# Splits of a norm, or of the mixer's output, woven into the first slabs of the product that reads them

## What is computed

```
for l in range(2):
    last = l == 1
    # context rows: all of it in layer 0, only the keys and values in layer 1
    hc = modulate(rms_norm_2(x_ctx, norm1_g[l]), cmod[0], cmod[1])
    hl = modulate(rms_norm_2(x_lat, norm1_g[l]), sh1, sc1)       # x * (1 + scale) + shift
    pa, q, k, v, pc = project(hl, P, rope)                       # hl @ w_in, 1024 x 2560
    o = diff_attn(q, k_all, v_all, lam)                          # 4 heads, two softmaxes each
    ya = chunk_gmlp(pa); yb = rms_norm_2(o, subln_g) * c; yc = conformer_conv(pc)
    x_lat = x_lat + g1 * (concat([ya, yb, yc]) @ w_out)          # 1024 x 1024
    h2 = modulate(rms_norm_2(x_lat, norm2_g[l]), sh2, sc2)
    x_lat = x_lat + g2 * ((silu(dwconv(h2 @ w_gate)) * (h2 @ w_val)) @ w_down)   # 2816 wide
```

## Time and profile before

| what | value |
|---|---|
| median of 3 runs | 2446.95 us |
| lowest and highest run | 2436.7 and 2447.53 us |
| profiled execution | 2444.05 us, of it the span 2442.4 us |
| TensorE matmul busy | 2222.0 us, 91% of the span |
| VectorE, ScalarE, GpSimd busy | 58%, 44%, 12% |
| mean granted TensorE clock | 0.948 of full speed |
| second block | from about 1348 us to the end |

### The profile page before, as it was taken

One profiled execution on the slowest core, in us unless ns is written; L12 is line 12 of the kernel. 1 busy time (PEld: TensorE's weight loads), 2 busy tenths in 40 slices (PEclk: granted clock), 3 DMA queues, 4 the chain that ended last, 5 costly groups with the idle time before them and its releaser, 6 DMA issues. The chain is left out here.

```text
span 2442.4 us, 31205 instructions
## 1 busy us (share of the span) xinstructions
PE 2222.0 (91%) x11948; PEld 1803.7 (74%) x11948; DVE 1421.3 (58%) x2234; ACT 1063.3 (44%) x1753; POOL 304.7 (12%) x310
## 2 busy tenths in 40 slices
PE   8998999899999989899999797789999998778999
PEld 6776677778777766777787675567888886658987
DVE  4655485554456555755454598755555337866664
ACT  4444555444344434554444454523232225454342
POOL 0007121100000062221000073100000001500000
PEclk9998999999999989999999898789999999889999
DMA  7553334466556534345656321222333334234654
GB/s 234 185 179 133 117 129 142 157 214 203 199 188 210 167 118 142 97 144 175 236 170 192 130 69 52 70 69 70 104 129 97 124 99 147 69 105 131 202 174 149
DMA packets 171842, 349.28 MB, mean 143 GB/s; under 512 B 11824, under 2 KB 23216, under 8 KB 171696
## 3 DMA queue, kind: packets, MB, share of 16 engines
q1 hardware_dynamic: 171696, 347.29, 43.7%
HBM read 346.19 MB, written 1.05 MB: 142 GB/s over the span
## 5 line engine op out<-in xcount | busy, mean ns | idle before, releaser
L820 DVE TENSOR_TENSOR wlo<-wraw,whi 128x1024 fp32r<-128x1024 f32 (+1 forms) x538 | 646.0, 1214 | 712.9 <-ACT whi L1017 710.9
L1017 ACT ACTIVATE whi<-wraw 128x1024 fp32r<-128x1024 f32 (+1 forms) x552 | 557.7, 1026 | 603.7 <-PE psum L1773 280.0
L1773 PE MATMUL psum<-whi,act_h 128*128 128x512 f32 (+2 forms) x1424 | 578.7, 406 | 30.4 <-DVE wlo L820 21.8
L1773 PE MATMUL psum<-wlo,act_h 128*128 128x512 f32 (+2 forms) x1424 | 557.4, 391 | 0.0
L1773 PE MATMUL psum<-whi,act_l 128*128 128x512 f32 (+2 forms) x1424 | 557.1, 391 | 0.0
L1773 PEld LDWEIGHTS psum<-whi,act_h 128*128 128x128 f32 x1424 | 275.6, 194 | 100.2 <-DVE wlo L820 25.6
L1773 PEld LDWEIGHTS psum<-whi,act_l 128*128 128x128 f32 x1424 | 274.4, 193 | 57.7
L1773 PEld LDWEIGHTS psum<-wlo,act_h 128*128 128x128 f32 x1424 | 275.4, 193 | 48.7
L1773 PE MATMUL psum<-act_h,whi 128*128 128x512 f32 (+1 forms) x704 | 243.8, 346 | 14.8 <-DVE cacc L1395 6.3
L1773 PE MATMUL psum<-act_l,whi 128*128 128x512 f32 (+1 forms) x704 | 239.6, 340 | 0.0
L1773 PE MATMUL psum<-act_h,wlo 128*128 128x512 f32 (+1 forms) x704 | 239.1, 340 | 0.0
(11 more groups left out here) (268 smaller groups left out, 2772.8 us busy)
## 6 DMA issues: line engine op xcount, KB each, us to landing
wraw<-in_w_in SPq DMA_DIRECT2D x136, 512.0 KB, 4.4
wraw<-in_w_gate SPq DMA_DIRECT2D x104, 512.0 KB, 4.2
wraw<-in_w_mod_pieces SPq DMA_DIRECT2D x96, 512.0 KB, 4.7
wraw<-in_w_ffn_in SPq DMA_DIRECT2D x80, 512.0 KB, 4.4
wraw<-in_w_ffn_out SPq DMA_DIRECT2D x44, 512.0 KB, 4.1
wraw<-in_w_down SPq DMA_DIRECT2D x44, 512.0 KB, 4.3
wraw<-in_w_val SPq DMA_DIRECT2D x40, 512.0 KB, 4.2
wraw<-in_w_branch SPq DMA_DIRECT2D x32, 512.0 KB, 4.8
```

The source lines that it names most:

```text
L820: eng.tensor_tensor(wlo[:, i, 0:st.n, 0:st.w], wraw[:, st.s % RING_W, 0:st.n, 0:st.w], whi[:, i, 0:st.n, 0:st.w].bitcast(F32), ALU.subtrac ...
L1017: nc.scalar.activation(whi[:, d % RING_S, 0:st.n, 0:st.w], wraw[:, s % RING_W, 0:st.n, 0:st.w], ACT.Copy).then_inc(sem("slab_rounded"), 1)
L1773: return nc.tensor.matmul(out, lhsT, rhs, start=start, stop=stop)
```

## The change

The splits are no longer all ahead of the product: four stand before its first slab, two before the second, two before the third (`between`), at all six places. `w_out_2` takes its slabs in the order in which its splits are made, k = 0, 6, 2, 4 (`order`), in both column groups. The count of product banks is set to 0 ahead of the feed-forward part, so that the first group of `w_gate_2` has banks 0 to 3, which no split uses; all later groups rotate from there. By the same count `w_down_2` then begins with banks 0 and 1, the banks of the last group of `w_val_2`, in both layers. In the attention, `subln`, `subln_root` and `subln_scale` move from right behind `att2_v` to the end of the round, behind `att2_t`, `att2_e` and `att2_m`. The number and shape of the instructions and loads are the same.

```diff
-def gemm(pl, weight, layer, act, tiles, nk, col0, width, evac, row0=0, kt0=0, ready=(), turned=False, **more):
+def gemm(pl, weight, layer, act, tiles, nk, col0, width, evac, row0=0, kt0=0, ready=(), turned=False, order=None, **more):
 
     steps = []
+    order = order or range(0, nk, SLAB_K)
...
-        for k in range(0, nk, SLAB_K):
+        for at, k in enumerate(order):
             n = min(SLAB_K, nk - k)
-            last = k + n == nk
+            last = at == len(order) - 1
...
-            pl.steps += ss
-            return {st.k: [("mod_lo", st.lo)] for st in ss}
-
-        ready = norm(0, 4, l > 0)
+            return {st.k: [("mod_lo", st.lo)] for st in ss}, between(ss)
+
+        def between(ss):
+
+            return [(0, st) for st in ss[:4]] + [(1, st) for st in ss[4:6]] + [(2, st) for st in ss[6:]]
+
+        ready, ss = norm(0, 4, l > 0)
...
-        others = [(5, cglu), (6, ct)] + [(at, st) for at, st in zip((7, 7, 11, 12, 12, 17, 17, 18), parts)]
+        others = ss + [(5, cglu), (6, ct)] + [(at, st) for at, st in zip((7, 7, 11, 12, 12, 17, 17, 18), parts)]
...
         for i in range(len(units) + 3):
+            behind = []
...
                 if kind == "att2_v":
-                    att += pending[:1]
+                    behind += pending[:1]
                     del pending[:1]
                     if h == B_HEADS - 1:
                         subs.append(Step(kind="subln", l=l, t=t, n=pl.tick("subs"), waits=drained(st.banks[0])))
-                        att.append(subs[-1])
+                        behind.append(subs[-1])
                         for part in ("subln_root", "subln_scale"):
                             pending.append(Step(kind=part, l=l, t=t, n=subs[-1].n))
+            att += behind
         att += pending
...
-            pl.steps += out
-
-        residual("w_out_2", "act2", KD, 0, {st.k: drained(st.bank) for st in ss}, True)
-
-
-        ready = norm(1, T, True)
+            pl.steps += weave(out, others)
+
+        residual("w_out_2", "act2", KD, 0, {st.k: drained(st.bank) for st in ss}, True, between(ss), order[::SLAB_K])
+
+
+        ready, ss = norm(1, T, True)
         pl.mod_queue, pl.mod_every, pl.mod_since = [(l, c) for c in MOD_GATES[1]], 5, 0
         base = pl.now("hid_lo")
-        pl.turns = tuple(range(7))
+        pl.turns, pl.gemm_banks = tuple(range(7)), 0
         for c, (a, w) in enumerate(widths(FFN)):
             n0 = pl.now("hid_lo")
             for weight, evac in (("w_gate_2", "ffg"), ("w_val_2", "ffv")):
-                pl.steps += gemm(pl, weight, l, "act2", T, KD, a, w, evac, ready=ready, turned=True, n0=n0)
-                ready = ()
+                pl.steps += weave(gemm(pl, weight, l, "act2", T, KD, a, w, evac, ready=ready, turned=True, n0=n0), ss)
+                ready = ss = ()
```

More of the change, by code:

```diff
@@ L171, in gemm @@
             banks.append(pl.gemm_bank())
-        for k in range(0, nk, SLAB_K):
+        for at, k in enumerate(order):
             n = min(SLAB_K, nk - k)
-            last = k + n == nk
+            last = at == len(order) - 1
             st = Step(kind="slab", s=len(pl.slabs), weight=weight, layer=layer, row=row0 + k, n=n, col=col0 + a, w=w,
-                      act=act, kt=kt0 + k, tiles=tiles, banks=banks, first=k == 0, last=last, c=c, a=a, evac=evac,
+                      act=act, kt=kt0 + k, tiles=tiles, banks=banks, first=at == 0, last=last, c=c, a=a, evac=evac,
                       turned=turned, **more)
@@ L181, in gemm @@
                 st.ready = [w for i in range(n) for w in ready.get(k + i, [])]
-            elif c == 0 and k == 0:
+            elif c == 0 and at == 0:
                 st.ready = list(ready)
@@ L197, in gemm @@
             elif (pl.mod_queue or pl.mod_last) and tiles == 2 and st.s >= 3 * RING_W:
-                at, slabs_in = k // SLAB_K, -(-nk // SLAB_K)
-                if pl.mod_queue and at % 4 == 0 and at + 3 < slabs_in:
+                if pl.mod_queue and at % 4 == 0 and at + 3 < len(order):
                     st.after = mod_ride(pl, pl.next_bank())
@@ L540, in plan_second, with residual @@
                    hi=pl.tick("split2_hi")) for k in order]
-        pl.steps += ss
-        def residual(weight, act, nk, g, ready, summed):
-            out = gemm(pl, weight, l, act, T, nk, 0, D, "res", ready=ready, g=g)
+        def residual(weight, act, nk, g, ready, summed, others=(), order=None):
+            out = gemm(pl, weight, l, act, T, nk, 0, D, "res", ready=ready, g=g, order=order)
             for st in out:
```

## The result

| | before | after |
|---|---|---|
| median of 20 runs | 2438.82 us | 2448.66 us |
| lowest and highest | 2429.39 and 2447.53 | 2443.7 and 2460.91 |
| span of the profiled execution | 2442.4 | 2447.8 |
| mean granted TensorE clock | 0.948 | 0.951 |

The changed kernel takes 1.0038 of the time of the one before, 95% interval 1.0027 to 1.0049: 9.3 us more (6.6 to 12.0). So the change is real, and smaller than the half per cent (12.2 us) that the prediction took as the least that tells from no change.

A forecast was written before the change was run, and what follows sets the result against it. TensorE, busy for 91% of the span, was taken as the bound, with VectorE the slower engine in the splits. The terms +4.5 - 4.5 + 3.0 + 1.8 + 0.35 + 1.9 - 4.0 made +3.0 us on 2446.95: 2450 us, range 2438 to 2460.

The forecast's parts named there:

- the band to which I gave 0.5: Whole kernel: 2445 to 2453 us, with no two terms at their far ends; chance 0.5.
- the clock rival: Woven products: broken starts keep TensorE at 1.2 GHz a whole slab longer than taken; +12.4, 2459 us; chance 0.1.
- first `w_in_2`: Layer 0: start 1.6 us earlier, two chains 4.8 later, clock 1.25 slower; sum 4.5 us slower.
- first `w_gate_2` and `w_down_2`: Layer 0: `w_gate_2` net 4.5 us faster, its slab 0 starting 8.1 earlier; `w_down_2` 0.5 later for a bank's drain.
- second `w_in_2`: Start 1.6 us earlier, slab 3's 1.2 delay gone, chains of 3.05 and 2.85, nothing for the clock; net 3.0 slower.
- second `w_gate_2` and `w_down_2`: Layer 1: `w_gate_2` 1.8 us slower from two chains of 1.45; `w_down_2` 1.4 later, waiting for a bank's drain.
- attention and `w_out_2`, twice: Attention 4 us faster from its new order; `w_out_2` 0.25 slower at the first place, 0.1 at the second.
- The chains: Slabs 1 and 2 wait for transposes, scaling and low part of a split; 2.4 us each at four tiles.
- The start of slab 0: Behind norms: 1.6 us earlier at each `w_in_2`, 8.1 at the first `w_gate_2`, 1.1 at the second.
- The clock: Slab 0: 1.25 us lost at the first `w_in_2`, 1.25 gained at the first `w_gate_2`, nothing at the second `w_in_2`.
- Attention: Copy `aT` and exponentials go ahead of the sub-norm's squares, so TensorE waits less for `aT`; 4 us faster, 9.3 at most.
- `w_down_2`: Its first bank is the last `w_val_2` group's and must drain first; 0.5 us later in layer 0, 1.4 in layer 1.

The follow-up runs named there:

- E11: Changed kernel, but VectorE makes the low parts of blocks 3 and 5 in their own steps, not those of blocks 4 and 6; 0.9993 of the kernel before.
- E7: Changed kernel with the transposes of block 3 of every norm issued three times, output the same; 1.0010 of the kernel before.
- E5: Changed kernel with five splits ahead of slab 0, two ahead of slab 1, one ahead of slab 2, at all six places; 0.9966 of the kernel before.
- E2: Kernel before with only own banks for the first group of `w_gate_2`, nothing woven, old attention order; 0.9968 of the kernel before.
- E3: Kernel before with only the attention order changed, sub-norm and its scaling behind the steps of their round; 0.9981 of the kernel before.
- E1: Changed kernel with all eight splits ahead of slab 0 again at both `w_in_2`, other places still woven; 0.9993 of the kernel before.
- E4: Kernel before with own banks for `w_gate_2`, the new attention order and `w_down_2` from its third bank, nothing woven; 0.9934 of the kernel before.
- E6: Changed kernel with `w_down_2` begun from the third of its four banks, nothing else; 1.0007 of the kernel before.

## Why the prediction was right

It was right in sign and in class: slower, by less than half a per cent. The size was not right: +3.0 us was forecast, +9.3 (6.6 to 12.0) measured. That the time itself, 2448.66, lies 1.3 us from the forecast 2450 is luck, since the median of the kernel before moved from 2446.95 to 2438.82 with more runs. Counted from that median, the band to which I gave 0.5 reaches to 6 us slower, and the measured difference lies above it, nearer to the 12.4 of the clock rival than to the 3.0. By the terms of its sum:

| term | forecast | profiles |
|---|---|---|
| first `w_in_2` | +4.5 | +5.1 |
| first `w_gate_2` and `w_down_2` | -4.5 + 0.5 | -1.9 |
| second `w_in_2` | +3.0 | +4.1 |
| second `w_gate_2` and `w_down_2` | +1.8 + 1.4 | +2.9 |
| attention and `w_out_2`, twice | -4.0 + 0.35 | -4.0 |
| between `w_in_2` and the attention | 0 | +1.3 |

**The chains were right**, 2.4 us each at four tiles (2.39 in the timeline), and for the reason named: the low part of block 3 stands in the step of block 4. E11 took that place away and the pauses went. The start of slab 0 was right at all four places behind a norm.

**The clock was mis-sized, and it is the step that is off most.** I took 1.25 us of loss at the first `w_in_2`, 1.25 of gain at the first `w_gate_2`, and nothing at the second `w_in_2`, because its clock rises while the first four splits are being transposed. It did so before; in the changed kernel it stood at 0.50 until 9 us behind the first transposes. E7 measures what the pauses cost the changed kernel: 1.7, 2.7 and 1.3 us. The largest error is at `w_gate_2`: I took half of the 2.5 us that slab 0 lost before as won, and it lost 2.7 again. Forecast for the three places by the clock: 1.25 - 1.25 + 0 = 0; against before the profiles have 1.6 + 0.2 + 1.3 (the last by E7) = 3.1 us. Two thirds of the 4.6 us by which the profiles miss the sum are this. The rival of the clock had the right place and a price too high: no slab lost more than 2.8 us, and slabs 1 and 2, which its sign wanted at 0.50, had the full clock.

**What weaving can win I did not ask.** I wrote that the transposes of splits five to eight stand in time in which TensorE would wait anyway, and charged their time as a part of each chain. What I didn't draw from it is that with four tiles weaving has nothing to win even without chains: slab 0 starts 1.6 us sooner, and sixteen moved transposes take the 1.6 back (E11). With no pause left it came out within 0.3 us of the splits ahead where the clock was full, and 1.4 behind where it was not (E5). Nor did I see that own banks give their 8.1 us alone (E2), so that the change's one large gain has nothing to do with the weaving.

**Attention**: 4 us forecast, 3.1 + 3.0 in the profiles with splits ahead, a ratio of 0.9981 alone. The size was near, the reason was not. I expected fewer waits for `aT`; these went from 9.3 us to 11.9, and 11.2 in E3. The waits that fell are those for `e`, to 4.5 us from these:

```profile
PE psum L1776 <- DVE e L1479: 13.0, 6, 4.5
```

VectorE mixes the exponentials in the step behind `att2_v`; before, it first bounded or scaled the values of a `subln` there. That this is the reason is argued, not shown: no run moves the work of VectorE and that of ScalarE separately.

**`w_down_2`** was right: 0.5 and 1.4 us forecast, a wait of 0.44 in layer 0, and in layer 1 the drain that I named, with 2.49 us of idle time but net 1.4 (70.3 us from the last wait for a low part to the end against 68.9). It is about 3 in E1, E2, E5 and E11 (71.8 to 72.2), where the clock fell behind the pause, as E2's windows show. E4 and E6 show that one number takes it away.

**Between `w_in_2` and the attention** nothing was forecast. Stretch W to S takes 65.7 to 67.3 us in the fourteen profiles, in no relation to an edit: E6, with the order of the changed kernel, has the shortest.

The Trainium skill ("TensorE: Matmul & The Clock Gate", Part 4: PE-mode transpose) says that the full clock doesn't engage for transposes and that they don't count as busy in the same way. E7 speaks against it again: eight more transposes, and slab 0 has the full clock.

## What to carry to other kernels

Before moving work of a busy engine behind something, look at what it does in that time now: here TensorE's transposes filled time in which it had to wait for VectorE, so that placed later they cost their full length, 0.8 us for eight, and the sixteen moved ones took all that the earlier start had won. Take a change with several parts apart before judging it: own banks, the attention's order and a better first bank for `w_down_2` took 17 us off the second block once the weaving was left out, while the two woven `w_in_2` alone cost 9. And where a step finishes the item before it, as the low part here, moving the step moves both.

## What the runs showed of the hardware

- The clock answers late. After sixteen transposes it was at 1.00, stayed there through 2.1 us without work, and fell to 0.50 one microsecond into slab 0, for 3 us. In E2 it fell behind a pause of 2.48 us, while the same pause in the changed kernel cost nothing; in E1 a pause of 1.86 us cost nothing where the changed kernel lost 2.7. Pauses of 1.0 to 2.2 us between transposes and product went with a loss of 0 to 2.8 us here.
- Filling such a pause with useless transposes gave back 5.7 us in three places of one program and 0.3 at a fourth, so useless work on the busiest engine can pay.
- Eight transposes of 128x128 between products hold TensorE up for 0.79 us at full clock, though the last ends 1.03 us behind the start of the first.
- Two profiles of one kernel agreed within 0.2 us in each of six stretches of 90 to 390 us, while the first 1350 us, the same code in all, varied by 12 us. The noise between these profiles lies largely there, and stretches tell more than spans.
